# Two small transposes moved from TensorE to VectorE, gate matmuls in four row groups, and the first parameters loaded with x

## What is computed

```python
def hybrid_layer(x, norm_g, w_in, a_sinks, w_oa, w_alpha, b_alpha, ...):
    h = rmsnorm(x, norm_g)                       # x * rsqrt(mean(x*x) + eps) * norm_g
    (qa, ka, va, ga, qb, kb, vb, ab, gb, cq, ckv, kr, gc, mg) = split_cols(h @ w_in)
    ya = swa_sink_attention(rope(qa), rope(ka), va, a_sinks) * silu(ga)
    log_a = log_sigmoid(ab @ w_alpha + b_alpha) / 16      # ab: 16 columns; log_a: 4 heads x 64
    yb = rmsnorm(gla_chunk_readout(qb, kb, vb, log_a), b_head_g) * silu(gb)
    k_rope = apply_rope(kr)                               # 32 columns, shared by the heads
    yc = mla_attention(q_nope, q_rope, k_nope, k_rope, v_c) * silu(gc)
    y = m0 * (ya @ w_oa) + m1 * (yb @ w_ob) + m2 * (yc @ w_oc)
    return x + y @ w_out
# and after the last layer rmsnorm(x, final_g)
```

## Time and profile before

| what | us |
|---|---|
| median of 3 runs (931.98 to 932.19) | 932.1 |
| the profiled execution | 931.54 |
| its span, first to last instruction | 929.7 |
| PE busy | 922.0 (99%) |
| DVE busy | 601.2 (65%) |
| ACT busy | 387.2 (42%) |
| mean granted TensorE clock | 0.999 of full |

### The profile page before, as it was taken

The page is one execution under the profiler, slowest core; times in us unless marked ns, Lnnn a source line. Parts: engine busy times, 40 slices in busy tenths (PEclk is TensorE's granted clock), DMA queues, the critical chain, the costliest instruction groups (busy, mean ns, idle before and its releaser), DMA issues.

```text
span 929.7 us, 13082 instructions
## 1 busy us (share of the span) xinstructions
PE 922.0 (99%) x5108; PEld 755.8 (81%) x5108; DVE 601.2 (65%) x982; ACT 387.2 (42%) x724; POOL 0.2 (0%) x4
## 2 busy tenths in 40 slices
PE   9999999999999999999999999999999999999997
PEld 7988888888888777888889888888888887778886
DVE  7856467448757877575457664674477568876834
ACT  7453344324543454432444333442264425562324
POOL 0000000000000000000000000000000000000000
PEclk9999999999999999999999999999999999999999
DMA  7324324322434255422232333253234433454542
GB/s 292 136 70 147 114 69 136 113 91 80 140 122 140 85 151 150 145 92 90 91 113 91 95 108 106 68 163 109 91 92 143 140 114 109 122 156 136 146 127 90
DMA packets 43789, 110.98 MB, mean 119 GB/s; under 512 B 8592, under 2 KB 11408, under 8 KB 43600
## 3 DMA queue, kind: packets, MB, share of 16 engines
q1 hardware_dynamic: 39664, 104.82, 35.8%
q10 hardware_dynamic: 4064, 5.33, 2.2%
HBM read 85.41 MB, written 2.23 MB: 94 GB/s over the span
## 4 chain that ended last, share of the span: by engine, by line
PE 86%; DVE 5%; ACT 3%; SPq 2%; issue 1%; DMA 1%; ACTq 1%; DVEq 0%
PE ring L657 65%; PE nat L657 9%; PE nat L868 3%; PE aux L892 2%; SPq L495 1%; DVE w_lo L1215 1%; ACT work L1117 1%; PE nat L672 1%; PE nat L671 1%; PE nat L673 1%; DVE work L1514 1%; DMA raw<-pieces 1%; ACT w_hi L909 1%; PE ring L672 1%; PE ring L671 1%
## 5 line engine op out<-in xcount | busy, mean ns | idle before, releaser
L657 PE MATMUL ring<-act_hi,w_hi 128*128 128x512 f32 x784 | 308.7, 394 | 0.0
L657 PE MATMUL ring<-act_lo,w_hi 128*128 128x512 f32 x784 | 305.5, 390 | 0.0
L657 PE MATMUL ring<-act_hi,w_lo 128*128 128x512 f32 x784 | 305.2, 389 | 0.0
L909 ACT ACTIVATE w_hi<-raw 128x1024 fp32r<-128x1024 f32 x152 | 161.7, 1064 | 340.5 <-PE ring L657 275.5
L1215 DVE TENSOR_TENSOR w_lo<-raw,w_hi 128x1024 fp32r<-128x1024 f32 x152 | 184.6, 1216 | 82.7 <-ACT w_hi L909 82.3
L657 PEld LDWEIGHTS ring<-act_hi,w_hi 128*128 128x128 f32 x784 | 147.1, 188 | 38.2 <-issue 8.4
L657 PEld LDWEIGHTS ring<-act_hi,w_lo 128*128 128x128 f32 x784 | 147.2, 188 | 31.1
L657 PEld LDWEIGHTS ring<-act_lo,w_hi 128*128 128x128 f32 x784 | 147.2, 188 | 29.7
L1545 DVE SCALAR_TENSOR_TENSOR gates<-ring,rstd 128x512 f32<-128x512 f32 x72 | 49.3, 685 | 77.0 <-PE ring L657 76.8
L657 PE MATMUL ring<-y_hi,w_hi 128*128 128x512 f32 x192 | 74.9, 390 | 0.0
L657 PE MATMUL ring<-y_hi,w_lo 128*128 128x512 f32 x192 | 74.7, 389 | 0.0
(11 more groups left out here) (227 smaller groups left out, 995.6 us busy)
## 6 DMA issues: line engine op xcount, KB each, us to landing
raw<-pieces SPq DMA_DIRECT2D x152, 512.0 KB, 3.5
bank_g<-work SPq DMA_DIRECT2D x120, 64.0 KB, 2.0
lat<-work SPq DMA_DIRECT2D x72, 64.0 KB, 2.0
bank_g<-work ACTq DMA_DIRECT2D x40, 64.0 KB, 2.2
xt<-x_t SPq DMA_DIRECT2D x8, 256.0 KB, 4.9
bank_a<-work SPq DMA_DIRECT2D x32, 64.0 KB, 2.0
bank_g<-bank_a SPq DMA_DIRECT2D x16, 128.0 KB, 3.9
out<-gates SPq DMA_DIRECT2D x7, 256.0 KB, 2.1
```

The costliest lines, as they stand in the source:

```text
L657: mm = pe.matmul(dst, stationary, moving, start=start and i == 0, stop=stop and i == 2)
L909: nc.scalar.activation(w_hi[:, n % HL, :], raw[:, n % RAW, :], ACT.Copy).then_inc(hi_split.sem, 1)
```

## The change

- `rstd_nat`: DVE turns `rstd` itself, in four transposes of 32 x 32 blocks (32 partitions x 128 each) into `y_pre`, and copies from there. PE has no part in it.
- `turn_ab`: DVE turns `k_ab` in sixteen 32 x 32 transposes into `ab1`, and then the key columns in four of 32 x 4 x 32 into `k_rot`. PE and ACT have no part. `k_ab` has 64 columns per token tile now, the last 16 set to one by a memset; tokens t*128 to t*128+127 come to rows 32t to 32t+31 of `ab1`.
- `gla_gate`: the four matmuls contract 32 partitions each, tile t from rows 32t on; `alpha_all` holds w_alpha and bias four times.
- DVE's three small instructions stand behind `rope_k` in both layers, the sinks behind a wait for the parameters.
- Layer 0: the gains of the first norm come as eight columns ahead of x's first tile in one transfer. The parameters are issued behind both weight quarters. The first quarter's `w_hi` is made by DVE. The split of piece 3 stands in `begin`, ahead of the last two squares and adds. Five warm-up matmuls in place of six.

```diff
-WARM = 6
+WARM = 5
-AUX = [s for s in SCHEDULE if s[0] in ("rms", "rstd_nat", "gla_end", "latent", "turn_ab")]
+AUX = [s for s in SCHEDULE if s[0] in ("rms", "gla_end", "latent")]
...
-                sp.dma_start(xt[:, j, :], x_t[:, j, :]).then_inc(x_loaded[j].sem, 16)
+                cols = slice(KT + j * S if j > 0 else 0, KT + j * S + S)
+                sp.dma_start(x_all[:, cols], x_t[:, cols]).then_inc(x_loaded[j].sem, 16)
...
                     elif name == "gla_gate":
-                        pe.wait_ge(ab_turned.sem, ab_turned.at(layer, 1))
+                        pe.wait_ge(ab_turned.sem, ab_turned.at(layer, 4 * TT))
                         pe.wait_ge(v_a_set.sem, v_a_set.at(layer, TT))
                         for t in range(TT):
-                            mm = pe.matmul(nat_gate[:, t, :], ab1[:, t * P:(t + 1) * P], alpha_all[:, layer, :],
-                                           start=True, stop=True)
+                            rows = slice(32 * t, 32 * t + 32)
+                            mm = pe.matmul(nat_gate[:, t, :], ab1[rows, 0:P], alpha_all[rows, layer, :], start=True, stop=True)
...
-                if n == 0:
-                    act.dma_start(par_all[:, :, :], params).then_inc(par_loaded.sem, 16)
+            act.dma_start(par_all[:, :, :], params).then_inc(par_loaded.sem, 16)
...
-            head_hi_part(0)
-            act.wait_ge(par_loaded.sem, 16)
...
                     if name == "begin":
+                        if layer == 0:
+                            split_hi(0, RAW)
...
-            dve.wait_ge(head_hi.sem, 1)
-            head_lo_half(*HEADS[0]).then_inc(head_lo.sem, 1)
+            p, cols = HEADS[0]
+            dve.wait_ge(head_loaded[0].sem, 16)
+            nc.vector.tensor_copy(w_hi[:, p, cols], raw[:, p, cols]).then_inc(first_hi.sem, 1)
+            dve.wait_ge(first_hi.sem, 1)
+            head_lo_half(p, cols).then_inc(head_lo.sem, 1)
...
                     elif name == "begin":
+                        if layer == 0:
+                            split_lo(0, RAW)
                         for n in range(1, LATE + 1):
                             add_square(layer, n)
+                    elif name == "rope_k":
+                        rope_k(layer)
+                        dve.wait_ge(par_loaded.sem, 16)
                         nc.vector.tensor_scalar(neg_sink[:, :], par_all[:, layer, SINKS:SINKS + A_HEADS], -1.0, None,
                                                 ALU.mult).then_inc(sink_neg.sem, 1)
                         nc.vector.memset(ab1, 1.0).then_inc(ones_row.sem, 1)
...
                     elif name == "rstd_nat":
-                        dve.wait_ge(aux_ready.sem, aux_ready.at(layer, u + 1))
-                        nc.vector.tensor_copy(rstd_nat[:, :], aux[:, :].rearrange("p (t n) -> p t n", t=TT)[:, :, 0]
-                                              ).then_inc(aux_free.sem, 1)
+                        turn = y_pre[:, 0:P].rearrange("p (t r) -> p t r", t=TT)
+                        dve.wait_ge(rstd_set.sem, rstd_set.at(layer, 1))
+                        for n in range(4):
+                            rows = slice(32 * n, 32 * n + 32)
+                            nc.vector.transpose(turn[rows], rstd[rows, :].rearrange("p (t n c) -> p t n c", t=TT, n=4)[:, :, n, :]
+                                                ).then_inc(rstd_turned.sem, 1)
+                        dve.wait_ge(rstd_turned.sem, rstd_turned.at(layer, 4))
+                        nc.vector.tensor_copy(rstd_nat[:, :], turn[:, :, 0]).then_inc(rstd_nat_set.sem, 1)
+                    elif name == "turn_ab":
+                        dve.wait_ge(ones_row.sem, ones_row.at(layer, 1))
+                        dve.wait_ge(k_ab_set.sem, k_ab_set.at(layer, TT + 1))
+                        dve.wait_ge(k_ab_rot.sem, k_ab_rot.at(layer, 2))
+                        for t in range(TT):
+                            for n in range(4):
+                                nc.vector.transpose(ab1[32 * t:32 * t + 32, 32 * n:32 * n + 32],
+                                                    k_ab[32 * n:32 * n + 32, t, 32:64]).then_inc(ab_turned.sem, 1)
+                        for n in range(4):
+                            nc.vector.transpose(k_rot.rearrange("p (t n r) -> p t n r", t=TT, n=4)[:, :, n, :],
+                                                k_ab[32 * n:32 * n + 32, :, 0:32]).then_inc(k_turned.sem, 1)
```

More of the change, by code:

```diff
@@ L943, in split_x @@
                 nc.scalar.activation(act_hi[:, j, :], xt[:, j, :], ACT.Copy,
[L944 removed]
+                                     scale=gain_of(layer, j)).then_inc(x_hi.sem, 1)
             def head_hi_part(n):
@@ L991, in _ @@
                         if p + HL < PIECES:
-                            split_hi(layer, p + HL)
+                            if (layer, p) != (0, 0):
+                                split_hi(layer, p + HL)
                         elif layer + 1 < DEPTH:
@@ L1240, in split_x @@
                 dve.wait_ge(x_hi.sem, x_hi.at(layer, j + 1))
-                nc.vector.scalar_tensor_tensor(act_lo[:, j, :], xt[:, j, :], par_all[:, layer, G_X + j:G_X + j + 1],
+                gain_x = first_gain[:, j:j + 1] if layer == 0 else par_all[:, layer, G_X + j:G_X + j + 1]
+                nc.vector.scalar_tensor_tensor(act_lo[:, j, :], xt[:, j, :], gain_x,
                                                act_hi[:, j, :].bitcast(F32), ALU.mult,
@@ L1261, in _, with rope_k @@
                 add_square(-1, n)
+            def rope_k(layer):
+                dve.wait_ge(proj_free.sem, proj_free.at(layer, by_dve(first_output(PX) + 1)))
+                for g in range(A_KV):
+                    rows = slice(32 * g, 32 * g + 32)
+                    nc.vector.tensor_tensor(k_a[64 * g:64 * g + 32, :], work[rows, 0, :], work[rows, 1, :],
+                                            ALU.subtract).then_inc(rope_out.sem, 1)
+                    nc.vector.tensor_tensor(k_a[64 * g + 32:64 * g + 64, :], work[rows, 2, :], work[rows, 3, :],
+                                            ALU.add).then_inc(rope_out.sem, 1)
             def add_first_rows():
@@ L1333, in _ @@
                         nc.vector.tensor_tensor(sq_sum, sq[0], sq[1], ALU.add).then_inc(lat_acc.sem, 1)
-                    elif name == "rope_k":
-                        dve.wait_ge(proj_free.sem, proj_free.at(layer, by_dve(first_output(PX) + 1)))
-                        for g in range(A_KV):
-                            rows = slice(32 * g, 32 * g + 32)
-                            nc.vector.tensor_tensor(k_a[64 * g:64 * g + 32, :], work[rows, 0, :], work[rows, 1, :],
-                                                    ALU.subtract).then_inc(rope_out.sem, 1)
-                            nc.vector.tensor_tensor(k_a[64 * g + 32:64 * g + 64, :], work[rows, 2, :], work[rows, 3, :],
-                                                    ALU.add).then_inc(rope_out.sem, 1)
                     elif name == "k_dec":
@@ L1532, in _ @@
                     elif name == "quarter" and i % 4 == 1:
-                        if (layer, i) != (0, 1) and i // 4 != PUKV:
+                        if (layer, i) not in ((0, 1), (0, 5)) and i // 4 != PUKV:
                             split_lo(layer, i // 4 + 2)
@@ L1751 @@
     rows = np.zeros((P, DEPTH, B_HEADS * B_DK), x.dtype)
-    rows[32:32 + B_RANK] = w_alpha.transpose(1, 0, 2)
-    rows[32 + B_RANK] = b_alpha
+    for t in range(TT):
+        rows[32 * t:32 * t + B_RANK] = w_alpha.transpose(1, 0, 2)
+        rows[32 * t + B_RANK] = b_alpha
     arrays = {
-        "x_t": np.ascontiguousarray(x[0].T.reshape(KT, P, S).transpose(1, 0, 2)),
+        "x_t": np.concatenate([norm_g[0].reshape(KT, P).T, x[0].T.reshape(KT, P, S).transpose(1, 0, 2).reshape(P, -1)], axis=1),
         "pieces": pack_pieces(w_in, w_oa, w_ob, w_oc, w_uq, w_ukv, w_out),
```

52 lines of the change are left out of this document (21 added, 31 removed).

## The result

| | before | after |
|---|---|---|
| median of 4 runs on one chip | 932.05 us | 938.83 us |
| lowest to highest | 931.98 to 932.19 | 938.71 to 938.96 |
| ratio, 95% interval | | 1.0076 (1.0063 to 1.0088) |
| the profiled execution: time, span | 931.54, 929.7 | 938.94, 937.1 |
| mean granted clock of TensorE | 0.999 | 0.993 |

The change makes the kernel 6.8 us slower. The prediction was 930.3 with a range up to 932.9, so both the sign and the range were wrong.

What follows compares the result with a forecast made beforehand. PE's own queue bounds the kernel, with DVE deciding when the gates start. Gains of 0.82 and 1.01 us at the two layers' gates sum to 1.8: 931.54-1.8=929.7, +0.56 gives 930.3, range 928.2 to 932.9.

Steps and rivals of the forecast that it cites:

- What bounds the kernel: Whole kernel: PE carries 86% of the chain; DVE's order before the gates decides, opening waits of 1.9 and 0.75 us.
- Sixteen 32x32 transposes. No row shows one. ... I take 0.11: DVE's turn of key and rank columns before the gates: 0.11 us each, 1.76 per layer, bounds 0.07 and 0.25.
- Rival 4: DVE's sixteen transposes before the gates: nothing overlaps, each takes 0.25 us, time 934.8; chance 0.10.
- 4 x 0.21 + 0.06 = 0.9: DVE's turn of rstd: four 32x128 transposes and a dependent copy in place of one copy, 0.9 us.
- Norm chain: Front of layer 0: DVE's norm chain starts at 28.0 instead of 27.79, with the adds not starting earlier.
- No term: PE's clock behind a new wait of 2 us: stays at the 2.4 GHz level, so nothing is added.
- Front: gain 0.7, and 0.29: Front of layer 0 on PE: first real matmul 0.7 us earlier, wait at piece 3 gone for 0.29 more.
- The gates: Gate matmuls with 32 contraction rows in their own row groups: 0.7 us per layer instead of 1.73.
- What stays hidden: Work beside PE's queue: subtraction has slack of 1.4 us or more; piece 6 waits 0 to 0.3, swallowed by the gate wait.

Runs made afterwards that it cites:

- h4: Kernel before with only the change's front, plus 120 unused DRAM columns so x's rows start at multiples of 512 bytes: 931.00 us against 931.81.
- h1: Changed kernel with one early in-place transpose for the sixteen, sixteen diagonal gate matmuls, x's DRAM rows aligned by 120 unused columns: 929.53 us against 931.81.
- e2: Changed kernel with 8 (layer 0) and 6 (layer 1) extra matmuls on constants before PE's wait for the gates' inputs: 934.78 us against 938.83.
- e1: Changed kernel with key and rank columns turned by PE and copied by ACT again, 128-row gate matmuls; rstd stays on DVE: 933.78 us, 931.97 before.
- g1: Changed kernel with only rstd turned by PE again, the sixteen transposes kept: median 933.67 us, three runs at 932.0 to 932.2, seven at 933.6 to 933.8.
- e3: Kernel before with only the change's front, both turns and the gates as before: 931.73 us against 931.97, ratio 0.9997.
- h3: Changed kernel with rstd turned by PE, plus 5 and 3 matmuls on constants before the gate waits: 932.07 us, all ten 932.02 to 932.17.

## Why the prediction was wrong

- **What bounds the kernel** was right: PE's own queue, and DVE's order up to the gates. The place of the new wait and its releaser were named and are there in both layers.
- **"Sixteen 32x32 transposes. No row shows one. ... I take 0.11"** is the first step that failed. Measured 0.233, 1.97 more in each layer. The step put the size on a line between two rows of transposes that all start at the same partition. But the trace of before had rows of DVE that change it: the rope of the keys (L1339, L1341) writes each time to a place 32 partitions further on. Its four instructions start 0.71 apart at 0.67 to 0.68 each, so nothing overlaps, while a product that stays in its group (L1316) starts 0.61 behind one of 0.69:

```profile
30.43 0.69 DVE L1315 TENSOR_TENSOR gates<-rope,rstd 128x512 f32<-128x512 f32 x1
31.04 0.68 DVE L1316 TENSOR_TENSOR gates<-rope,rstd 128x512 f32<-128x512 f32 x1
...
38.51 0.67 DVE L1339 TENSOR_TENSOR bank_a<-work 32x512 f32<-32x512 f32 x1
39.22 0.68 DVE L1341 TENSOR_TENSOR bank_a<-work 32x512 f32<-32x512 f32 x1
```

Rival 4, which says just this, stood at 0.10 with the remark that no row has it. With 0.233 in the prediction's own working the sum is 929.7+2x1.97 = 933.6 against 931.54 before: slower.
- **"4 x 0.21 + 0.06 = 0.9"** for rstd failed for the same reason: 0.33 each, 1.41 for the group, 0.4 to 0.5 too little in each layer.
- **"Norm chain"**: it was to start at 28.0, 0.2 late, and began at 28.72 in the changed kernel, 0.9 late. The step that the adds "hang on weight transfers that stay where they are" failed: the transfers moved, and with aligned rows the chain began at 27.97 (h4) and 28.00 (h1), as the working had it. Together with rstd this made the columns 1.0 later than the working had them (45.54 against 44.53 in layer 0).
- **"No term" for the clock** is the second large failure: 4.5 in the profile, 4.05 by e2. The step took its evidence from the first two microseconds behind PE's last matmul, which ended at about 924.0. The stretches just behind them, where PE stays idle, have the lower clock:

```profile
926.00:928.00 2.00, 0.00 (x0) 0.00 (x0) 0.53 (x2) 0.72 (x1) 0.00 (x0) 0.83 0.33 122
928.00:930.00 2.00, 0.00 (x0) 0.00 (x0) 0.00 (x0) 0.00 (x0) 0.00 (x0) 0.50 0.41 154
```

So the trace of before showed that a longer idleness costs PE its clock; that a wait of 2 us is safe did not follow from it. At waits of 1.9 and 0.9 (e1) two executions of ten were 1.7 slower, at 2.1 and 1.2 (g1) seven of ten were 1.6 slower, and at 3.9 and 2.9 all four took some 4 more than with the waits filled. The two errors are linked: a wait twice to four times as long as forecast (3.9 for 1.9, 2.9 for 0.75) is what made the clock's price full and certain.
- **"Front: gain 0.7, and 0.29"**: 0.24 in e3, 0.8 in h4. The working left out that "the first 32 bytes per partition longer" shifts every later row of x in DRAM. It also had x's first tile land at 4.23, as before; it landed at 4.5 to 5.0 with the new front, and the first ring matmul began at 5.38 to 5.93 for the 5.4 forecast.
- **The gates** were right: 0.71 in eight records at the full clock, predicted 0.7. Nothing in the runs speaks against the row groups.
- **What stays hidden**: piece 6 and the subtraction caused no wait of their own, as forecast.
- **Rival 4** is what happened, at a pitch of 0.233 where it had 0.25, and its 934.8 lies 4 us under the result, which is the clock. That e2, with the clock kept, took 934.78 is in part luck: the pitch is 0.5 too high over the thirty-two, and the late front and rstd are left out.

## What to carry to other kernels

Before cutting one DVE instruction into many small ones, look at the group of 32 partitions in which each starts: each change costs the overlap, here 0.1 us per instruction of 32 elements, and the trace of this kernel already had it in the rope of the keys. Where blocks must be turned, turn them in place over all 128 partitions (0.31 against 3.73) and let the matmul's position in the array do the moving, which cost 1.86 for the gates in place of 0.71 here. And price a new wait of PE twice, for its length and for the clock behind it: here the second was as large as the first.

## What the runs showed of the hardware

- In the changed kernel's profile TensorE's granted clock fell after 2.7 us of idleness in layer 0 (48.2 to about 50.9). In layer 1, after an idle of 2.9, it fell about a microsecond into the new work. Behind the last matmul of the kernel before (924.0) it stayed 1.00 until 926, was 0.83 in the mean of the next 2 us and 0.50 after. With waits of 2.1 and 1.2 (g1) seven executions of ten were 1.6 us slower, at a lower mean clock, and with 1.9 and 0.9 (e1) two of ten were 1.7 slower. In the changed kernel it came back 5.6 and 4.3 us after work had begun again (52.13 to about 57.7, 514.22 to about 518.5), with 2.8 and 1.8 us lost.
- Matmuls on constants in a wait of this kind paid for themselves: 14 of them gave 4.05 us back (e2), 8 gave 1.6 and took the spread from 1.8 to 0.15 us (h3).
- With rows of x 16416 bytes apart in DRAM, most of them starting at no multiple of 512 bytes, the DMA engines moved 2.58 to 2.63 MB in the first 10 us (eight profiles); with the rows at multiples of 512 bytes 2.78 to 2.81 MB (four profiles).
- Four transposes of 32x128 that change their group take 0.33 each. One of 128x128 in place takes 0.31, and back to back 0.21 each.
